# A two-layer S5 / RG-LRU / mLSTM transformer block on one core: loads moved within the queue, and other PSUM banks for the z tiles

## What is computed

```python
for l in range(2):
    h = rms_norm(x, norm_g[l]) * (1 + scale) + shift      # scale, shift, gate: silu(c) @ mod_w[l] + mod_b[l]
    o = even_mixer(h) if l == 0 else odd_mixer(h)
    x = x + gate * o
return rms_norm(x, final_g)

even_mixer: u, gs, xr, gr = split(h @ w_in)
    ys = S5 scan of u, both directions, 64 groups of 16 channels, 64 complex states each
    yr = RG-LRU of conv(xr), both directions, 4 heads of 256 channels
    y = gelu(ys + d * u);  y = y * sigmoid(y @ glu_w + glu_b)
    return concat([y * silu(gs), yr * silu(gr)]) @ w_out
odd_mixer: xm, z = split(h @ w_in)
    xcv = silu(conv(xm));  q, k = blockdiagonal(xcv);  v = blockdiagonal(xm)
    hm = mLSTM(q, k, v, gates), both directions, 4 heads of 512 channels
    return ((head_norm(hm) * g + skip * xcv) * silu(z)) @ w_out
```

## Time and profile before

| | |
|---|---|
| median of 3 runs | 2723.4 us (2722.6 to 2731.67) |
| the profiled execution, its own time | 2730.52 us |
| its span, from the first to the last instruction | 2728.9 us |
| busy: PE, PEld, DVE, ACT, POOL | 2568.9, 1988.9, 1539.2, 825.9, 1000.1 us |
| chain that ended last | PE 66%, DVE 11%, issue 3%, ACT 3%, DMA 2% |
| granted TensorE clock, mean | 0.974 of full speed |
| DMA | 298.15 MB, 109 GB/s over the span |

### The profile page before, as it was taken

The page is one execution under the profiler, slowest core; times in us unless marked ns, Lnnn a source line. Parts: engine busy times, 40 slices in busy tenths (PEclk is TensorE's granted clock), DMA queues, the critical chain, the costliest instruction groups (busy, mean ns, idle before and its releaser), DMA issues.

```text
span 2728.9 us, 37425 instructions
## 1 busy us (share of the span) xinstructions
PE 2568.9 (94%) x13319; PEld 1988.9 (73%) x13319; DVE 1539.2 (56%) x2362; ACT 825.9 (30%) x994; POOL 1000.1 (37%) x1162
## 2 busy tenths in 40 slices
PE   7897899999998998999999999989999999999998
PEld 2787764445444667888877887778989889898787
DVE  3677765887875225443227655876555654656510
ACT  2425544362643113222112111213324242322210
POOL 0139967887810110031233433444433433331000
PEclk9999999999999999999999999999999999999999
DMA  7413220101104877451123333564121320314421
GB/s 291 119 56 102 101 88 17 58 24 50 51 16 134 277 245 227 100 195 35 44 84 78 129 120 110 185 226 167 48 105 63 105 86 28 121 47 170 131 93 47
DMA packets 257493, 298.15 MB, mean 109 GB/s; under 512 B 34977, under 2 KB 217545, under 8 KB 256977
## 3 DMA queue, kind: packets, MB, share of 16 engines
q1 hardware_dynamic: 202672, 211.85, 24.2%
q10 hardware_dynamic: 50080, 67.80, 6.9%
q0 software_dynamic: 4608, 16.78, 1.8%
HBM read 203.09 MB, written 93.29 MB: 109 GB/s over the span
## 4 chain that ended last, share of the span: by engine, by line
PE 66%; DVE 11%; issue 3%; ACT 3%; DMA 2%; ACTq 0%; POOL 0%; SPq 0%; DVEq 0%; POOLq 0%
PE ps L136 58%; PE ps L1350 6%; DVE xc_part L2511 1%; DVE s_scan_tmp L2217 1%; DVE s_scan_tmp L2215 1%; DMA weights<-in_e_w_in 1%; DVE arena L2219 1%; PE ps L1002 1%; DVE arena L2269 1%; ACT L1545 0%; DVE arena L2237 0%; PE ps L1355 0%; ACT arena L1545 0%; DVE arena L526 0%; DVE arena L2262 0%
## 5 line engine op out<-in xcount | busy, mean ns | idle before, releaser
L136 PE MATMUL ps<-h_full,weights 128*128 128x512 f32 (+1 forms) x1152 | 421.6, 527 | 16.6 <-DMA weights<-in_e_w_in 9.2
L136 PE MATMUL ps<-h_part,in_weight_parts 128*128 128x512 f32 (+1 forms) x1920 | 412.3, 375 | 8.7 <-DVE h_part L1987 5.5
L136 PEld LDWEIGHTS ps<-h_part,in_weight_parts 128*128 128x128 f32 x1920 | 336.9, 190 | 79.1 <-issue 7.8
L136 PEld LDWEIGHTS ps<-h_full,weights 128*128 128x128 f32 x1152 | 219.7, 192 | 212.2 <-issue 186.3
L136 PE MATMUL ps<-v_part,p_part 128*128 128x512 f32 x1248 | 298.3, 398 | 0.1
L136 PEld LDWEIGHTS ps<-v_part,p_part 128*128 128x128 f32 x1248 | 236.5, 192 | 50.2 <-issue 0.8
L136 PE MATMUL ps<-q_part,xc_part 128*128 128x256 f32 x1920 | 243.8, 285 | 3.9 <-DVE q_part L2544 3.9
L136 PEld LDWEIGHTS ps<-q_part,xc_part 128*128 128x128 f32 x1920 | 233.5, 191 | 4.9 <-DVE q_part L2544 4.5
L136 PE MATMUL ps<-arena,weights 64*16 64x128 f32 (+2 forms) x896 | 184.1, 408 | 17.7 <-ACT arena L1545 14.4
L1350 PE MATMUL ps<-wo_part,mx_part 128*128 128x512 f32 x768 | 184.0, 400 | 5.0 <-DVE mx_part L2511 4.5
L2848 POOL TENSOR_TENSOR in_weight_parts<-weights,ones 128x1024 fp32r<-128x1024 f32 x32 | 82.0, 2563 | 263.6 <-PE ps L136 187.6
(11 more groups left out here) (394 smaller groups left out, 4213.6 us busy)
## 6 DMA issues: line engine op xcount, KB each, us to landing
weights<-in_e_w_in SPq DMA_DIRECT2D x32, 512.0 KB, 5.2
weights<-in_o_w_in SPq DMA_DIRECT2D x32, 512.0 KB, 4.2
arena<-in_mod_w POOLq DMA_DIRECT2D x24, 512.0 KB, 6.2
s_out_maps<-arena ACTq DMA_DIRECT2D x16, 640.0 KB, 2.9
arena<-s_out_maps SPq DMA_DIRECT2D x16, 640.0 KB, 5.6
ml_xcv<-arena ACTq DMA_DIRECT2D x16, 640.0 KB, 2.9
xc_full<-ml_xcv SPq DMA_DIRECT2D x4, 2560.0 KB, 9.9
xm_tiles<-ml_xm SPq DMA_DIRECT2D x16, 640.0 KB, 3.8
```

The costliest lines, as they stand in the source:

```text
L136: return nc.tensor.matmul(o, lhsT, rhs, start=(k == 0), stop=(k == n - 1))
```

## The change

The edits, in the order of the file (the waits are as in the diff; what is left out repeats signatures):

```diff
-        Mb = [... for o in (2560, 3072, 16128)]
-        Fu = [... for o in (3584, 4224, 13312)]
+        Mb = [... for o in (2560, 3712, 16128)]
+        Fu = [... for o in (3072, 4224, 13312)]
...
-        Z_BANKS = (0, 3, 0, 3, 0, 6, 3, 0, 6, 3, 0, 3, 5, 0, 3, 5)
+        Z_BANKS = (0, 2, 0, 2, 4, 6, 0, 2, 4, 6, 0, 2, 0, 6, 2, 4)
...
+        Xm0 = W[:, 0:TOK]
...
@@ SP, start of the S5 output stage
             for z in range(2):
                 gate_weight(0, z)
-            branch_out(RH - 1)
             sp.wait_ge(*past("g_stored0", 16 * NB // 2))
             sp.wait_ge(*past("g_stored1", 16 * NB // 2))
-            map_rows(0, 0)
-            with sp.Fori(0, NB // 4 - 1) as i:
+            for s in range(2):
+                sp.wait_ge(*past(f"rg_gmm{s}", 4 * RH))
+            sp.wait_ge(*past("rg_bo", 2 * RH - 1))
+            batch_rows(0, 0, "f_in0")
+            gate_weight(1, 0)
+            sp.wait_ge(*past("rg_bo", 2 * RH))
+            batch_rows(1, 1, "f_in1")
+            branch_out(RH - 1)
+            for i in range(NB // 4 - 1):
                 for z in range(2):
-                    gate_weight(i + 1, z)
+                    if i or z:
+                        gate_weight(i + 1, z)
                     map_rows(i + z, 1 - z)
@@ SP, end of that stage
             batch_rows(NB - 2, 2, "f_in2")
-            sp.wait_ge(*past("f_mm0", NB // 2 - 1))
-            batch_rows(NB - 1, 0, "f_in3")
             sp.wait_ge(*past("gs_mm1", 12))
...
                 sp.dma_start(YF32[:, k0:k0 + n], ...).then_inc(sem(f"y_in{q}"), 16)
-                if q == 0:
+                if q == 1:
+                    sp.wait_ge(*past("f_mm0", NB // 2 - 1))
+                    batch_rows(NB - 1, 0, "f_in3")
+                elif q == 2:
                     glu_weight(1)
@@ SP, output product
-            sp.wait_ge(*past("glu_ao", DT))
-            sp.wait_ge(*past("bo_stored", 16 * RH))
-            for q in range(4):
+            def branch_rows(q):
                 sp.dma_start(BF32[:, 2 * q:2 * q + 2], ...).then_inc(sem(f"bo_in{q}"), 16)
-            for h in range(2):
-                with sp.Fori(1 - h, DT // 2) as i:
-                    for s in range(2):
-                        sp.wait_ge(*past("eo_wl", 2 * i + (DT * h + s - 1)))
-                        sp.dma_start(Wv[:, s], ...).then_inc(sem(f"eo_w{s}"), 16)
+            def next_mix_weights(h, i, s):
+                sp.wait_ge(*past("eo_wl", 2 * i + (DT * h + s - 1)))
+                sp.dma_start(Wv[:, s], ...).then_inc(sem(f"eo_w{s}"), 16)
+            for i in range(1, DT // 2):
+                for s in range(2):
+                    next_mix_weights(0, i, s)
+                    if i == 1 and s == 0:
+                        sp.wait_ge(*past("glu_ao", DT))
+                        sp.wait_ge(*past("bo_stored", 16 * RH))
+                    if i < 3:
+                        branch_rows(2 * i + s - 2)
+            with sp.Fori(0, DT // 2) as i:
+                for s in range(2):
+                    next_mix_weights(1, i, s)
@@ SP, before the first mLSTM head
             for s in range(2):
                 sp.wait_ge(*past(f"xm_stored{s}", 32 * MT // 2))
+                sp.wait_ge(*past(f"xz_split{s}", MT))
+            sp.dma_start(Xm0, xm_d[0]).then_inc(sem("xm_in0"), 16)
+            for s in range(2):
                 sp.wait_ge(*past(f"xz_mm{s}", MT))
-            for k in range(2):
-                value_rows(0, k)
+            value_rows(0, 1)
+            sp.wait_ge(*past("lo_mm", slot_done(0, "v", 2)))
             for s in range(2):
-                sp.wait_ge(*past(f"xz_split{s}", MT))
...
             mixing_rows(0, 0)
@@ PE, z tiles
-                elif m == 5:
+                elif m == 4:
                     pe.wait_ge(*past("rows_ready", 2))
-                elif m == 12:
+                elif m == 13:
                     pe.wait_ge(*past("em_free", 2))
...
-                if m == 9:
-                    pe.wait_ge(*past("z_ev", 9))
+                if m == 11:
+                    pe.wait_ge(*past("z_ev", 10))
...
-                    mm(ps[:, 2, 0:40], ones[0:64, :], TR...).then_inc(sem("rows_t"), 1)
+                    mm(ps[:, 7, P:P + 40], ones[0:64, :], TR...).then_inc(sem("rows_t"), 1)
@@ PE, values: the first block of head 0 reads Xm0 instead of Xm[:, 0]
@@ ACT, end of the S5 output stage
-            outputs_taken(NB // 4 - 1, 1, 0)
             for k in range(2):
                 outputs_high(k)
+            outputs_taken(NB // 4 - 1, 1, 0)
+            outputs_high(2)
             outputs_taken(NB // 4 - 1, 1, 1)
             for s in range(2):
                 outputs_stored(NB // 4 - 1, 1, s)
-            outputs_high(2)
@@ ACT, z tiles: the exponentials of the rows (L1816, L1817) after tile 9 instead of 7, the stores of the rows (L1821) after tile 10 instead of 8
@@ DVE, z tiles
-            gate_tile(7)
-            gate_tile(8)
+            for m in range(7, 11):
+                gate_tile(m)
             dve.wait_ge(*past("rows_t", 1))
...
-            V.tensor_copy(TB, ps[:, 2, 0:40]...)
+            V.tensor_copy(TB, ps[:, 7, P:P + 40]...)
...
-            gate_tile(9)
+            gate_tile(11)
...
-            for m in range(10, MT):
+            for m in range(12, MT):
```

More of the change, by code:

```diff
@@ L283, in build @@
         Fgv = [f.rearrange("p (g r k h) -> p g r k h", g=GB, r=2, h=HC) for f in Fgs]
-        Mb = [rb(o, 512).rearrange("p (g c) -> p g c", g=GB) for o in (2560, 3072, 16128)]
-        Fu = [rb(o, 640).rearrange("p (g j) -> p g j", g=GB) for o in (3584, 4224, 13312)]
+        Mb = [rb(o, 512).rearrange("p (g c) -> p g c", g=GB) for o in (2560, 3712, 16128)]
+        Fu = [rb(o, 640).rearrange("p (g j) -> p g j", g=GB) for o in (3072, 4224, 13312)]
         Zb = rb(4864, 2560).rearrange("p (s r g j) -> p s r g j", s=2, r=2, g=GB)
@@ L654, in _ @@
                 sp.dma_start(XT[:, 4 * q:4 * q + 4], xt_d.rearrange("p (k t) -> p k t", k=DT)[:, 4 * q:4 * q + 4]).then_inc(sem(f"xt_in{q}"), 16)
[L655 to L657 removed]
+            def branch_rows(q):
                 sp.dma_start(BF32[:, 2 * q:2 * q + 2], bo_d[2 * q:2 * q + 2].rearrange("k p t -> p k t")).then_inc(sem(f"bo_in{q}"), 16)
[L659 to L663 removed]
+            def next_mix_weights(h, i, s):
+                sp.wait_ge(*past("eo_wl", 2 * i + (DT * h + s - 1)))
+                sp.dma_start(Wv[:, s], ew_out[h, bass.ds(2 * i + s, 1)].rearrange("m p k n -> p (m k) n")).then_inc(sem(f"eo_w{s}"), 16)
+            for i in range(1, DT // 2):
[9 more added lines that the diff above has]
+                    next_mix_weights(1, i, s)
             def input_weight(i, s):
@@ L1219, in value @@
                 o = slot(i, "v", n)
+                x = Xm0 if isinstance(i, int) and i == 0 and k == 0 else Xm[:, k % 2]
                 for b in range(4 * c, min(4 * c + 4, NBLK)):
-                    last = mm(o[:, P * (b % 4):P * (b % 4) + P], Xm[:, k % 2, P * b:P * b + P], BDv[k % 2], 0, 1)
+                    last = mm(o[:, P * (b % 4):P * (b % 4) + P], x[:, P * b:P * b + P], BDv[k % 2], 0, 1)
                 last.then_inc(sem("lo_mm"), 1)
@@ L1337, in _ @@
                     pe.wait_ge(*past("tr_ready", 1))
-                    mm(ps[:, 2, 0:40], ones[0:64, :], TR.rearrange("p d h j -> p (d h j)"), 0, 1).then_inc(sem("rows_t"), 1)
+                    mm(ps[:, 7, P:P + 40], ones[0:64, :], TR.rearrange("p d h j -> p (d h j)"), 0, 1).then_inc(sem("rows_t"), 1)
             queries(0, 1)
@@ L1812, in _ @@
                     nc.scalar.activation(rA, rA, ACT.Exp, scale=-1.0).then_inc(sem("lf_exp"), 1)
-                elif m == 7:
+                elif m == 9:
                     act.wait_ge(*past("m_ready", 1))
@@ L1817, in _ @@
                     nc.scalar.activation(rA[32:64, 0:LAT][:, ::-1], rM[32:64, CTX:TOK], ACT.Exp, scale=-1.0).then_inc(sem("em_ready"), 1)
-                elif m == 8:
+                elif m == 10:
                     act.wait_ge(*past("xr_ready", 1))
@@ L2485, in _ @@
                     V.tensor_copy(flat[:, j::NBLK + 2], yt[:, j::2, 32 * d:32 * d + MH])
-            V.tensor_copy(TB, ps[:, 2, 0:40].rearrange("p (d h j) -> p d h j", d=2, h=MH))
+            V.tensor_copy(TB, ps[:, 7, P:P + 40].rearrange("p (d h j) -> p d h j", d=2, h=MH))
             V.tensor_copy(EMT, ps[:, 5].rearrange("p (j d c) -> p j d c", j=LBLK, d=2)[:, :, :, 0:MH]).then_inc(sem("em_free"), 1)
             dve.wait_ge(*past("em_free", 2))
-            gate_tile(9)
+            gate_tile(11)
             for q in range(QB - 1):
```

1 line of the change is left out of this document (removed).

## The result

Measured side by side, the kernel before ran at 2730.0 us (median of 5) and the changed one at 2709.3 (median of 5, 2705.4 to 2713.2): ratio 0.9934, 95% interval 0.9919 to 0.9949. It is faster, and inside the stated range, but by about 18 us by that ratio (the two medians are 20.7 apart) and not by 24. Later sets put the kernel before at 2727.0 to 2727.6, so single microseconds can't be read in medians. They can be read in the traces, if each part has its own stretch of PE's time. The profiled span went from 2728.9 to 2711.6, -17.3, of which 2.6 stood before any edit reached PE (the 48 records in front of the first stall began at 838.60 before and at 835.98 after).

What follows compares the result with a forecast made beforehand. TensorE, busy 94% of the span, was taken to bound the kernel. The terms -13.3 + 1 - 5.1 - 6.7 + 0 summed to -24.1 us, from 2723.4 to a median of 2699.3, range 2690 to 2711.

Steps and rivals of the forecast that it cites:

- What bounds it: Whole kernel: TensorE's queue sets the end, busy 94% of the span; a change pays only where that queue stands still.
- Part 1: Map rows in the last recurrent head: batch 0 and gate weight issued earlier, -13.3 us, bounds -11.3 and -13.3.
- Part 3: Branch reads spread between output weights: the weight of output tile 2 goes out first, -5.1 us, bounds -3.5 and -5.3.
- Part 5: First values read early into the weight buffer: second block still waits for bank 7, 0 us, bounds -0.6 and +0.3.
- Part 2: S5 output: two y reads ahead of the last rows, ACT's third y tile earlier; +1 us, bounds -3 and +3.
- PE then does outputs 15 until 1052: S5 output: after rows landing at 1048.5 to 1050, PE finishes the last outputs at 1052; y tile 3 ready about 1061.8.
- The -3: S5 output, good bound: last rows not delayed at all by the early y reads, gain of 2 to 3 us.
- Part 4: Four bank pairs for z, transposes two tiles later: 9.2 us saved, tile 14 wait 2.5; -6.7, bounds -9.5 and -3.
- PE waits 0 to 5; I take 2.5, the middle: z tile 14: its weight, queued behind column and decay rows, is split and ready at 1849 to 1856; PE wants 1851.0.
- the second rival: Transfer backlog served strictly in issue order everywhere: sum -16.4 us, time 2707.0, chance 0.2.
- The slower: SP's in-order queue at z tile 13 delays the weights of tiles 14 and 15: +13.1 us, 2736.5, chance 0.02.
- taken-back cases: S5 stage becomes bound by its transfers and takes back 11 us of the recurrent-head gain: -13.1, 2710.3, chance 0.07.

Runs made afterwards that it cites:

- e8: The kernel before with only the edits to the map rows inside the last recurrent head; 2712.6 us, ratio 0.9946.
- e4: Changed kernel with bank 7 read out earlier: ACT's query part before its last z store, DVE's before the last skip product; 2711.4 us, ratio 0.9944.
- e2: Changed kernel with SP's last batch's rows put back in front of the y reads, ACT's new order kept; 2704.1 us, ratio 0.9914.
- e9: Changed kernel with one y read instead of two in front of the last batch's rows on SP; 2705.9 us, ratio 0.9918.
- e3: Changed kernel with the weight of z tile 14 sent by SP in front of the column and decay rows; 2706.0 us, ratio 0.9927.
- e10: Changed kernel with all four branch reads put back in front of the weights; 2716.2 us, ratio 0.9959.
- e5: e3 with the query map also read by SP in front of the last skip row; 2702.3 us, ratio 0.9901.
- e6: e5 with the skip row of tile 12 also read in front of the column and decay rows; 2702.5 us, ratio 0.9904.

## Why the prediction was right and wrong

**What bounds it: right.** Everything gained came from PE's idle time and the slow records behind it, and what PE gained in one place stayed to the end. One reading was wrong, though nothing in the sum rests on it: PE's longest wait for a transfer is not the 8.1 us of the earlier trace rows but 13.06, for the conv weights at the start of the span.

**Part 1: right.** 13.6 in both traces and alone in e8, where the sum had 13.3; the store sent later cost nothing. **Part 3: right.** 5.3, with 5.1 forecast, and 6.9 by undoing it. **Part 5: right**, 0, for the reason given (bank 7). e4 shows that ACT's order was a second holder behind it, which I hadn't named.

**Part 2: right mechanism, wrong size, outside its bounds.** I had the rows landing at 1048.5 to 1050 on the time scale of the trace before; they landed at 1033.48, which is 1049.2 on it (B's start moved by 15.72). The step that failed is the next one: "PE then does outputs 15 until 1052". It took 24 records at 3.53; they took 5.92, until 1039.4, that is 1055.1 on the time scale of before, because PE came back at half clock. The rest of the chain (ACT's eviction and stores, weight, y part) followed as written, and tile 3 was ready at 1064.0 instead of 1061.8; PE's records behind it ran at half clock once more (0.58 from 1048 to 1052). So +1 became +4.1. The -3 that stood as the other bound needed early y reads and rows that aren't delayed; no run has both, and ACT's new order without the early reads is worth 0 (e2). The Trainium skill (DMA: Bandwidth & Descriptors, Queues, rings and completion order) has a descriptor that stands behind others in its ring taken up behind them. The dose of e9 agrees: 0, 3.5 and 7.2 us for none, one and two reads in front.

**Part 4: right mechanism, wrong size, outside its bounds too (1.6, where they were 3 to 9.5), and here is most of the miss.** Saved, as forecast, was 9.2. The step that failed is "PE waits 0 to 5; I take 2.5, the middle". Measured were 4.54 for POOL's split (the weight landed 16 us after its issue, just above the 15.5 taken as the worst), 2.6 for the half clock behind it (22.0 against 19.4), and 0.55 for the map: 7.7, not 2.5, and 9.2 - 7.7 is the 1.5 found. I had the trace's own price for such a surcharge in hand, and charged it to the stalls removed (2.27 in the earlier trace rows, 1.55 in the earlier trace rows, 1.35 in the earlier trace rows) but not to the ones I forecast. With such a price in both new waits, and the measured 4.54 for tile 14 in place of 2.5, the sum would have been -24.1 + 2.4 (outputs at half clock, as measured) + 2.0 + 2.3 (tile 14) = -17.4, or 2706, which is the 2707.0 of the second rival, the backlog served strictly in order. That rival was the better reading of the earlier trace rows, and part 4's map, which none of my cases had, would have capped the good end: without tile 14's wait PE still had 4.5 to pay (e3).

**The time itself** came out 10.0 us above the 2699.3 of the forecast. The terms account for 6 of that; the other 4 are the base: the 2723.4 of three runs lay below the 2727.0 to 2727.6 of the larger sets.

**The slower and the taken-back cases** didn't occur: no landing came near 37 us, and the S5 stage kept its length.

## What to carry to other kernels

A stall on PE costs its length and often slow records behind it (1.5 to 2.9 us behind the stalls of 3.5 to 8.1 us here); charge that to each stall a change removes, and to each it makes. Behind a wait stands the next one, often ready only a little earlier: before counting a wait as saved, look up when each further input of the next products arrives, and who issues its transfer. Where a queue is moved, the bytes in front of a load divided by the rate of that stretch are a fair estimate of its delay (3.5 us for each 1311 KB in e9), so send small loads that PE needs soon ahead of large ones that it needs late.

## What the runs showed that I had not expected

**The clock behind a short wait.** Waits of 3.52 and 7.17 us both brought the granted clock to 0.50 and cost about the same behind them (24 records in 6.37 and 5.92 for 3.5); waits of 0.55 and 0.67 left it at 1.00 (e4: 24 records in 3.11). So at its place a wait of 3.5 cost 6.4, and one of 7.2 cost 9.6. The length of the wait alone doesn't decide: behind the transposes, a wait of 1.20 in e3 was followed by records at full pace, and one of 1.35 in e10 by a granted clock of 0.50 (1819 to 1822) and 96 records in 23.87 instead of 22.36.

**DVE beside POOL.** The same four column parts took 10.28 us in e5 and 5.70 in e6. Windows over those stretches (busy time of PE, PEld, DVE, ACT, POOL in turn), e5 first, then e6:

```profile
1836.20:1846.40 10.20, 10.20 (x46) 8.20 (x45) 10.20 (x5) 1.03 (x1) 10.11 (x7) 1.00 0.49 166
```

```profile
1831.30:1837.00 5.70, 5.70 (x26) 4.66 (x25) 5.64 (x5) 4.54 (x5) 0.44 (x1) 1.00 1.06 388
```

In e5 POOL was busy all the while, with the split of tile 15's weight and the masks behind it; in e6 it stood idle. DVE took nearly twice as long beside POOL. All fourteen traces divide this way: 10.22 to 10.29 us in the nine in which POOL was at work beside these four parts, 5.68 to 5.70 in the five in which it stood idle or nearly so. The transfers don't divide them: the kernel before took 5.68 at 110 GB/s, e6 5.70 at 388, e5 10.28 at 166. No run was made for this alone, so that POOL is the cause is the likely reading and not shown.
